# Final norm inside the last feed-forward block, the next part's first weights beside it, and a new order of the opening's loads

## What is computed

```
for l in range(2):
    mod = silu(c) @ ada_w[l] + ada_b[l]          # six rows of 1024 ("ada")
    h = rms_norm(x, norm_mix_g[l]) * (1 + sc_m) + sh_m
    x = x + g_m * (attention_branches(h @ w_in[l], na_rpb[l]) @ w_out[l])
    h = rms_norm(x, norm_ffn_g[l]) * (1 + sc_f) + sh_f
    gate, up = split(h @ ffn_w_gate_up[l])       # 2816 wide each, 11 blocks of 256
    x = x + g_f * ((silu(gate) * up) @ ffn_w_down[l])
x = rms_norm(x, final_norm_g)                    # the final norm
```

## Time and profile before

| | |
|---|---|
| median of 3 executions | 1818.21 us (1813.79 to 1821.91) |
| profiled execution, its own time | 1813.24 us |
| span of its instructions | 1811.3 us |
| PE busy | 1604.7 us (89%) |
| DVE busy | 1227.2 us (68%) |
| ACT busy | 816.4 us (45%) |
| mean granted TensorE clock | 0.946 |
| read from HBM | 345.29 MB, 192 GB/s over the span |

### The profile page before, as it was taken

One profiled execution on the slowest core, in us unless ns is written; L12 is line 12 of the kernel. 1 busy time (PEld: TensorE's weight loads), 2 busy tenths in 40 slices (PEclk: granted clock), 3 DMA queues, 4 the chain that ended last, 5 costly groups with the idle time before them and its releaser, 6 DMA issues. The chain is left out here.

```text
span 1811.3 us, 25509 instructions
## 1 busy us (share of the span) xinstructions
PE 1604.7 (89%) x10701; PEld 1449.5 (80%) x10701; DVE 1227.2 (68%) x1354; ACT 816.4 (45%) x943; POOL 42.4 (2%) x60
## 2 busy tenths in 40 slices
PE   2899998999899998999969997897798958999995
PEld 2789887999798988899958997886686857888884
DVE  4877586988757557665554875534575757899895
ACT  1345533434344553443323662225433327777773
POOL 0100000000100000000000000000000000000000
PEclk9999999999999999999979998987887969999998
DMA  8975446999844324666245553111222447999992
GB/s 302 318 231 163 140 140 189 351 324 328 251 147 134 108 89 147 218 228 214 93 156 178 157 169 93 47 47 47 79 85 71 139 142 255 374 349 366 365 345 106
DMA packets 226057, 348.07 MB, mean 192 GB/s; under 512 B 14612, under 2 KB 156672, under 8 KB 225808
## 3 DMA queue, kind: packets, MB, share of 16 engines
q1 hardware_dynamic: 225936, 346.36, 57.1%
HBM read 345.29 MB, written 1.97 MB: 192 GB/s over the span
## 5 line engine op out<-in xcount | busy, mean ns | idle before, releaser
L459 PE MATMUL bank<-layer_split,hT_pair 128*128 128x256 f32 (+2 forms) x4032 | 512.7, 287 | 31.3 <-DVE hT_pair L1031 21.6
L459 PEld LDWEIGHTS bank<-layer_split,hT_pair 128*128 128x128 f32 x4032 | 486.2, 190 | 45.2 <-issue 29.9
L184 DVE TENSOR_TENSOR layer_split<-layer_raw,layer_split 128x2048 fp32r<-128x2048 f32 x122 | 279.6, 2292 | 100.8 <-ACT layer_split L172 99.4
L172 ACT ACTIVATE layer_split<-layer_raw 128x2048 fp32r<-128x2048 f32 x122 | 233.5, 1914 | 195.1 <-PE bank L459 73.7
L184 DVE TENSOR_TENSOR expert_split<-expert_raw,expert_split 128x2048 fp32r<-128x2048 f32 x96 | 219.5, 2290 | 40.7 <-ACT expert_split L172 40.6
L172 ACT ACTIVATE expert_split<-expert_raw 128x2048 fp32r<-128x2048 f32 x96 | 184.2, 1920 | 76.2 <-PE bank L2385 39.3
L459 PE MATMUL bank<-split_w,hT_pair 128*128 128x256 f32 (+1 forms) x1248 | 180.8, 308 | 13.6 <-PEq L2580 5.0
L459 PEld LDWEIGHTS bank<-split_w,hT_pair 128*128 128x128 f32 x1248 | 170.5, 204 | 24.3 <-issue 18.7
L184 DVE TENSOR_TENSOR split_w<-raw_w,split_w 128x2048 fp32r<-128x2048 f32 x52 | 119.2, 2293 | 66.2 <-ACT split_w L172 65.6
L1894 PE MATMUL bank<-layer_split,ffnh_aT 128*128 128x512 f32 x528 | 127.0, 396 | 2.8 <-DVE ffnh_aT L1962 2.8
L172 ACT ACTIVATE split_w<-raw_w 128x2048 fp32r<-128x2048 f32 x52 | 99.4, 1912 | 59.2 <-PE bank L459 50.7
(11 more groups left out here) (455 smaller groups left out, 1756.4 us busy)
## 6 DMA issues: line engine op xcount, KB each, us to landing
layer_raw<-in_ada_w SPq DMA_DIRECT2D x48, 1024.0 KB, 6.9
layer_raw<-in_ffn_w_gate_up SPq DMA_DIRECT2D x44, 1024.0 KB, 5.6
raw_w<-in_w_in SPq DMA_DIRECT2D x40, 1024.0 KB, 5.1
layer_raw<-in_w_in SPq DMA_DIRECT2D x38, 1024.0 KB, 6.1
expert_raw<-in_w_gate SPq DMA_DIRECT2D x32, 1024.0 KB, 7.1
expert_raw<-in_w_up SPq DMA_DIRECT2D x32, 1024.0 KB, 7.2
expert_raw<-in_w_down SPq DMA_DIRECT2D x32, 1024.0 KB, 6.9
layer_raw<-in_ffn_w_down SPq DMA_DIRECT2D x22, 1024.0 KB, 5.4
```

The source lines that it names most:

```text
L172: self.nc.scalar.activation(self.pair[:, j % self.pairs, 0, 0:self.size[n]], self.raw[:, n % self.depth, 0:self.size[n]], ACT.Copy).then_i ...
L184: self.nc.vector.tensor_tensor(self.pair[:, j % self.pairs, 1, 0:self.size[n]], self.raw[:, n % self.depth, 0:self.size[n]], self.pair[:, ...
L459: ins = nc.tensor.matmul(out, lhs, rhs, start=first and c == chunks[0] and tp + wp == 0, stop=last and c == chunks[-1] and tp == 1)
```

## The change

Five edits go together.

- **Feed-forward.** `turn(0)` is issued after the gate half of `hidden(1)` in both layers; the other turns stay where they are.
- **Final norm.** It becomes `RowNorm`, a `SkewNorm` with a row gain, and runs tile by tile at the end of layer 1's feed-forward, as the other norms do. Its gain is loaded in `rows_ahead`.
- **First weights.** The second part's ring is made first; its raw slots lie where `branch_gates` lay and its split slots where two of three `layer_split` slots lay. `rows_ahead` of layer 1 queues its first three units. ACT and DVE split unit 0 before the additions of the last block and unit 1 after the norm, before the Block ends.
- **Opening.** Units 8 to 10 are queued ahead of the gate row and the strips. POOL's mask also waits for two of the projection's DVE outputs, in both layers.
- **Constants and semaphores.** The last 276 columns of the constants are loaded a second time before the router, ahead of the two rows, because the first copy's room is freed. Several semaphores are shared between stages.

```diff
@@ constants: "sb_strict" moves behind "restart16"
@@ layers
+                LAYER[0] = ""
+                gain_loaded = new_sem(nc, "final_gain_loaded")
+                mix_norm.append(RowNorm("final", buf.junk, gate_rows[:, 0, :], (gain_loaded, 16)))
...
                     def rows_ahead(sp, l=l, merge=merge):
                         sp.wait_ge(merge.out_left.sem, 8)
+                        if l + 1 == DEPTH:
+                            sp.dma_start(gate_rows[:, 0, :], A["final_norm_g"].rearrange("(o n) -> o n", o=1)
+                                         .broadcast_to([P, D])).then_inc(gain_loaded, 16)
+                            second_ring.feed(sp, -1)
                         if l + 1 < DEPTH:
                             load_gate_row(sp, l + 1, 2, rows_loaded)
                             make_strips(sp, l + 1)
                         load_gate_row(sp, l, 5, rows_loaded)
@@ new
+        class RowNorm(SkewNorm):
+            def __init__(self, tag, junk, gain, gain_ready):
+                super().__init__(tag, [x[:, t, :] for t in range(TILES)], junk, gain, None, gain_ready)
+                self.copied = steps["dve"]
+            def norm(self, dve, t):
+                dve.wait_ge(*self.scale_ready)
+                dve.wait_ge(self.rooted.sem, 3 * (t + 1))
+                nc.vector.scalar_tensor_tensor(x[:, t, :], x[:, t, :], rstat[:, 4 + t:5 + t], self.scale, ALU.mult, ALU.mult) \
+                    .then_inc(self.normed, 1)
+            def part(self, t, half):
+                cut = (slice(None), slice(4 * half, 4 * half + 4), slice(t * P, (t + 1) * P))
+                return hP[:, 0, :, :][cut], hP[:, 1, :, :][cut], hT[:, :, :][cut], \
+                    ps[4 + 2 * t + half][:, :].rearrange("p (k s) -> p k s", k=4)
+            def flat(self, act, t):
+                for half in range(2):
+                    hi, lo, flat, src = self.part(t, half)
+                    act.wait_ge(self.turned, 2 * t + half + 1)
+                    nc.scalar.activation(hi, src, ACT.Copy).then_inc(self.flat_out, 1)
+            def vector(self, dve, t):
+                for half in range(2):
+                    hi, lo, flat, src = self.part(t, half)
+                    dve.wait_ge(self.flat_out, 2 * t + half + 1)
+                    done(dve, nc.vector.tensor_copy(flat, src), self.copied)
+                    nc.vector.tensor_tensor(lo, flat, hi.bitcast(FP), ALU.subtract).then_inc(self.lo_out, 1)
@@ Projection.sync, layer 0
-                    ring.feed(sp, ring.group_end[1] - ring.depth)
+                    ring.feed(sp, w["proj"][3] - ring.depth)
                     self.load_gate_row(sp)
                     self.make_strips(sp, 0)
@@ Projection.gpsimd
-                pool.wait_ge(self.bias_loaded, 64)
+                pool.wait_ge(self.bias_loaded, 64 * (self.l + 1))
+                pool.wait_ge(self.dve_out.sem, 2)
@@ FeedForward.tensor
                     for up, t in ((0, 0), (1, 0), (0, 1), (1, 1)) if n == 0 else ((0, 0), (0, 1), (1, 0), (1, 1)):
                         hidden(n, up, t)
+                        if n == 1 and (up, t) == (0, 1):
+                            turn(0)
...
                     if n >= 1:
                         down(n - 1)
-                    turn(n)
+                        turn(n)
                 down(blocks - 1)
+                if self.ring_next is not None:
+                    self.norm_next.turn(pe, 0)
+                    self.norm_next.turn(pe, 1)
@@ FeedForward.scalar, after the blocks
+                if self.ring_next is not None:
+                    act.wait_ge(ring.used, ring.uses(dn(self.blocks - 2)))
+                    self.ring_next.hi(act, 0)
+                for t, half in ((0, 0), (0, 1), (1, 0), (1, 1)):
+                    self.norm_next.square(act, t, half)
+                for t in range(TILES):
+                    self.norm_next.flat(act, t)
+                if self.ring_next is not None:
+                    self.ring_next.hi(act, 1)
@@ FeedForward.vector, after the blocks
+                if self.ring_next is not None:
+                    self.ring_next.lo(dve, 0)
                 dve.wait_ge(self.tile_sum, 1)
                 self.add(dve, 0, 0)
...
+                norm.vector(dve, 0)
+                norm.norm(dve, 1)
+                norm.vector(dve, 1)
+                if self.ring_next is not None:
+                    self.ring_next.lo(dve, 1)
@@ normalize_and_route
+                        sp.dma_start(tables["second"][:, :], A["constants"][:, tables["from"]:width]).then_inc(router_in, 16)
                         for i, name in enumerate(("ln1_g_2", "ln1_b_2")):
@@ mixer: class Norm is gone
-                norm = Norm("final", s2, ring, U_A[0], row_gain=gain[:, :], late_gain=(gain_loaded, 16), junk=work_[:, 0, :])
-                project("mix_in", ring, jobs, banks=7, norm=norm,
+                project("mix_in", ring, jobs, banks=7,
```

More of the change, by code:

```diff
@@ L238, in program @@
         cst = sb("cst", [P, first_width])
-        tables = {"first": cst}
+        tables = {"first": cst, "from": first_width}
+        steps = {}
         def const(name):
@@ L244, in const @@
                 return cst[:, at:at + n]
-            return tables["second"][:, at - first_width:at - first_width + n]
+            return tables["second"][:, at - tables["from"]:at - tables["from"] + n]
         ident, ones = const("ident"), const("ones")
@@ L990, in __init__ @@
                 self.added = None
-                self.rooted, self.split = (Count(nc, f"{tag}_{n}") for n in ("rooted", "split"))
+                self.rooted, self.split = Count(nc, f"{tag}_rooted"), steps["dve"]
                 self.squared = [Count(nc, f"{tag}_tile_{t}_squared") for t in range(TILES)]
@@ L1833, in program, with __init__ @@
         class FeedForward:
-            def __init__(self, ring, w, blocks, buf, norm, norm_next, ada, rows_ahead, gate):
+            def __init__(self, ring, w, blocks, buf, norm, norm_next, ada, rows_ahead, gate, ring_next):
+                self.ring_next = ring_next
                 self.ring, self.w, self.blocks, self.buf, self.norm, self.norm_next, self.ada, self.rows_ahead, self.gate = \
@@ L1931, in scalar @@
                         ring.hi(act, ring.ahead(dn(n - 1), 3))
-                if self.norm_next is not None:
-                    for t, half in ((0, 0), (0, 1), (1, 0), (1, 1)):
-                        self.norm_next.square(act, t, half)
-                    for t in range(TILES):
-                        self.norm_next.flat(act, t)
+                if self.ring_next is not None:
[7 more added lines that the diff above has]
+                    self.ring_next.hi(act, 1)
             def add(self, dve, t, half):
@@ L2100, in second_part, with run @@
                                        .rearrange("(k p) n -> p k n", p=P))
-            tables["second"] = sb("cst_second", [P, width - first_width])
-            with ExitStack() as st:
-                ring = Ring(nc, "second", sb("raw_w", [P, 3, UNIT], st), sb("split_w", [P, 2, 2, UNIT], st, FR), units)
+            second_ring = Ring(nc, "second", second_raw, second_split, units)
+            def run():
+                ring = second_ring
+                tables["second"] = sb("cst_second", [P, width - first_width], early)
@@ L2132, in scaled_add @@
+            return second_ring, run
         def scaled_add(tag, factor):
```

203 lines of the change are left out of this document (73 added, 130 removed).

## The result

The changed kernel takes 1825.07 us (median of 20, 1818.87 to 1834.06), the kernel before beside it 1818.14 (20 executions, 1811.65 to 1822.38). The ratio is 1.0045, 95% interval 1.0033 to 1.0057: slower by 8.2 us (6.0 to 10.4). Forecast was 1816.0, a gain of 2.2, within 1808 to 1824; the result lies above that range. The profiled execution has a span of 1825.9 us against 1811.3; that pair lies 14.6 apart, and part of it is chance, as will be seen. Lines have moved: L387 is the products' line (L459 before), L1869 down, L1857 turn, L1943 and L1946 DVE's two products of a block, L970 the norm's low half.

The account below looks back on a forecast made before the run. PE was taken as the bound in the feed-forwards after two blocks, DMA in the opening, chained single instructions at the handover. Terms -2.8 - 0.4 + 2.0 - 2.7 + 1.1 + 0.6 = -2.2 us gave 1816.0, range 1808 to 1824.

Parts of the forecast that it names:

- Opening: Start of the kernel: units 8 to 10 ahead of the strips fill DMA holes, net -2.8 us; bounds -6.2 and 0.
- the strips' move: Opening's DMA queue: strips now go at about 39 us, at share 0.58 for 4.5 us, costing 2.0 us.
- the opening gives nothing: Rival for the opening: the queue from 56 us on is full anyway, total 1818.8; chance 0.15.
- Mask: Layer 1's norm low half: without POOL's mask beside it 0.69 instead of 1.10 us, so first projection product earlier, -0.4 us.
- turn(0) in layer 0: Layer 0 feed-forward: PE stands 5.5 us ahead of turn(1) and falls to half clock, +2.0 us; bounds 0 and 2.2.
- turn(0) in layer 1: Layer 1 feed-forward: PE's idle time of 2.67 us at turn(0) goes, -2.7 us if the added transfers do no harm.
- this rival's 1826.6: Rival: early loads starve layer 1's feed-forward, PE waits 6.3 us for gu(2, 1), total 1826.6; chance 0.09.
- Handover: From layer 1's last down to the second part: PE starts at 933.9 instead of 932.83, +1.1 us; bounds -1.2 and +1.9.
- the meeting of all engines: Block's end at the handover: from the last addition to the next Block's first instruction, 2.1 us.
- Constants: Before the router: the second load lengthens DVE's wait for the two rows, +0.6 us (0.4 to 0.8).

Follow-up runs that it names:

- b_second64: Kernel before with the second part's split_w and expert_split 64 bytes later, the tiles behind them 128 later; 1810.84 us, ratio 0.9969.
- a_handover: Changed kernel with the split of the second part's unit 1 left to the next Block, as before; 1824.02 us, ratio 1.0030.
- b_turn: Kernel before with the later turn(0) alone, in both layers; 1814.64 us, ratio 0.9996.
- b_best2: Kernel before with later turn(0) in both layers, gu(2, 0) queued ahead of layer 0's gate rows and strips, and tiles re-placed by distance; 1800.49 us, ratio 0.9909.
- b_both32: Kernel before with 32 bytes ahead of hT_pair, so that it and everything behind it move together; 1815.96 us, ratio 0.9983.
- a_place: Changed kernel with layer_split 32 bytes later and all tiles behind it 128 bytes later; 1823.02 us, ratio 1.0036.

## Why the prediction was wrong

- **Opening**, -2.8: wrong in mechanism too, no gain measured. The first product came 6.5 us earlier as forecast. The working counted the strips' move at 2.0 us but not their read-back, which moves forward with them. Unit 11, which was to come no later, was issued 3.9 us later, and the weights behind the read-back are queued no earlier. It was the rival "the opening gives nothing".
- **Mask**, -0.4: the low half beside it has 0.69 us as forecast; from the last down to layer 1's first product it is 8.0 to 8.8 us in kernels with the edit and 8.0 to 9.4 without, so the gain can't be told.
- **turn(0) in layer 0**, +2.0: right in mechanism and size (+2.2 alone). The trace agrees with what the prediction had weighed from the Trainium skill (TensorE: Matmul & The Clock Gate, "HAM oscillation"): behind the stand of 5.74 us turn(1) took 1.12 us, at half clock.
- **turn(0) in layer 1**, -2.7: right (-2.6), and more where the old stand happens to cost the clock (b_second64). The early loads starved nothing: PE did not wait in block 2. That the result lies near this rival's 1826.6 is chance, its mechanism did not occur.
- **Handover**, +1.1: measured 0.0. The chain of DVE is as written, with unit 1's low half as its last link (2.2 us, by a_handover); the meeting of all engines took 1.3 us from DVE's last instruction, where 2.1 had been carried over.
- **Constants**, +0.6: mis-sized, 2.9 on average of the traces. The wait grew by 1.7 in the profiled pair and by 0.9 on average, near the upper bound of 0.8. The rest is the half clock of the router's matmuls behind it, which the term had no place for.
- **What failed**: the sum had no term for where tiles lie. The move of layer_split, from byte 102720 to 76960, stood at nothing, without a reason; the runs put 6.2 us on it (4.2 + 4.2 - 2.2). The two feed-forwards lose 4.2 us each to it (6.4 - 2.2 and 1.6 + 2.6). The second part wins 2.2, since split_w too came to a better distance (its 2304 products are busy 321.5 us instead of 323.7). This term has the greatest size, and with the opening and the constants it turned a forecast gain into a loss.

Measured terms: 4.2 + 4.2 - 2.2 + 2.2 - 2.6 + 2.9 + 0 = 8.7, inside the 6.0 to 10.4 of the result; most terms are read from one or two traces each, so the agreement is no proof of each. The range ended at 1824, where its own terms gave 1823.1.

That the place is the cause is shown in both programs; why the distance acts so is not. Distances of 96, and what picks one of two paces where there are two, were not settled. Some of the spread from one execution to the next (11 us in the kernel before) may come from that choice and from stands that cost the clock in one execution and not in another; the traces, one for each kernel, can't show how much.

## What to carry to other kernels

An edit that moves a tile in SBUF can change the pace of every matmul that reads it: compare the start-to-start time of a full block without waits before looking at anything else, and try gaps of 32 bytes where PE is the bound. In a queue that holds a slow transfer, an earlier consumer only moves the wait to the unit behind it; b_turn and b_best2 differ in nothing else there. A wait added to a stand of PE is to be priced with the matmuls behind it at half clock. And a stage that is fast in one trace and slow in another is to be counted over all traces at hand before its cost is put down to an edit.

## What the runs showed of the hardware

The pace of a stream of fp32 products goes by the distance of its two operands modulo 256 bytes, from 113.3 to 120.0 ns for 256 columns (6%) and from 226.7 to 233.5 for 512 (3%), with both tiles 32 bytes later as before (b_both32), and at the same busy time of DVE and ACT. At some distances there are two steady paces. None of 301 full blocks of hidden that ran without a gap changed its pace; one of a_place that was held up once for 0.1 us (at 763 us) went from 113.3 to 117.8.

The Trainium skill (TensorE: Matmul & The Clock Gate, "Wait — 56ns, not 53.3ns?") gives the start-to-start time of warm matmuls as N / 2.4 GHz plus about 2.5 ns; worked out from that figure, an estimate for here is 109.2 and 215.8 ns. No run has it: the best are 113.3 and 226.7, and what is above it depends on the place.
